# Splitting mixer outputs beside the retention's matmuls instead of in a stage of their own

## The chip, the cores and the metric

The kernel runs on one core of a Trainium2 chip, as one launch. The metric is the device time of that launch in microseconds (us). A core has TensorE (matmuls), VectorE, ScalarE, GpSimd (POOL in the profile) and SyncE (SP, which here only starts transfers). They run side by side and meet only through semaphores.

## The reference, cut to what matters

Two model blocks run one after the other on x of 256 positions by 2048 channels. The first has two layers, and the change lies in these:

```python
for l in range(DEPTH):                       # DEPTH = 2
    u = rms_norm(h, norm_pre_mix[l])
    p = u @ w_in[l]
    p_ret, p_hgrn, p_ml, p_rw = split_cols(p, GROUP_COLS)
    o_ret = retention_group(p_ret)           # 512 channels each
    o_hgrn = hgrn2_group(p_hgrn, ...)
    o_ml = mlstm_group(p_ml, ...)
    o_rw, v_first = rwkv7_group(p_rw, ...)
    mixed = concatenate([o_ret, o_hgrn, o_ml, o_rw]) @ w_out[l]
    h = h + rms_norm(mixed, norm_post_mix[l])
    h = h + rms_norm(gated_ffn(h), norm_post_ffn[l])   # width 5632

def retention_group(p):
    q, k, v, g = split_cols(p, RET_SPLIT)
    o = chunked_retention(rotary(q), rotary(k) * HEAD_DIM ** -0.5, v)
    return head_rms(o) * silu(g)
```

All is float32. The second block (attention of two kinds, 2048 wide) is not touched.

## The kernel before

**Products in two parts.** Every large product is made from rounded numbers and their remainders. ScalarE copies a slab of weights to `w_hi` in a rounded format, then VectorE or GpSimd writes `w_lo`, the weights less `w_hi`. The activations are treated in the same way: `x_hi` (ScalarE) and `x_lo` (VectorE) are the two halves of `x_parts`, 16 tiles of 128 channels by 256 positions. TensorE adds hi times hi, hi times lo and lo times hi. "To split" below means this.

**Layout.** Channels lie on the 128 partitions, positions along the free dimension. Weight slabs come through a ring of four slots (`weight_ring`), filled by SyncE. `Linear` is a product with the machine to itself: chunks of four output tiles, its weight split one slab ahead, its epilogue on ScalarE and VectorE. `Woven` is a product cut into pieces of nine matmuls, each piece half of a slab for one output tile. The stages of the four mixers place these pieces by hand between their own small matmuls. A list of shares says how many pieces go into each place: `plan` takes it, and `weave.pe`, `weave.act`, `weave.pool` and `weave.sp` issue what each engine has to do for the pieces up to a step. ScalarE's part is to round the weights (L552 and L564 for the halves of a slab, L185 for a whole one) and to read out finished output tiles (L622). GpSimd's part is the remainders (L555, L567, L193). A finished slab frees its slot of `w_hi` and `w_lo`, so each piece depends on what ScalarE and GpSimd did a few pieces before.

**Order around the change, in each layer.** rwkv, hgrn, mlstm and retention run in this order, each with its head norm at its end. During one mixer the input projection of the next is woven in. During retention it is the first part of the output product instead: `out_rest`, the rows of `w_out` that belong to hgrn, mlstm and rwkv (tiles 4 to 15 of `x_parts`), 16 slabs, 64 pieces. Its result is written to the arena. After retention's head norm `out_ret`, a `Linear` of one slab a chunk and four chunks, adds the product with retention's own 512 channels (tiles 0 to 3).

Each stage is a block. A block ends when all engines have drained; the last to be done holds the next. Before the change the sequence is:

1. mlstm's head norm, with the last pieces of retention's projection.
2. `split_stage`, a block of its own: three ScalarE copies and three VectorE subtractions of 128 by 1024 split the outputs of the three mixers.
3. `retention_stage`. SyncE loads the cosine and sine table (256 KB) and the decay table (1536 KB), then weights. TensorE rotates q and k (L1475), transposes v (L1447), does 8 woven pieces, and waits for `qk_ready` and `v_ready`. Then come the scores (L1428, L1430) and the weighted values, with 8 pieces after each of the four head pairs and 3 at the end. ScalarE begins with the second slab of `out_rest` (`weave.open`), then evacuates v. VectorE waits for the tables and makes q and k in three operations (L1515, L1517, L1518).
4. `head_norm_stage` of the retention: ScalarE squares, TensorE sums, ScalarE takes the root, VectorE inverts it and multiplies (L1411, L1413). Shares `[3, 64]`: 3 pieces before the sums, the rest (18) behind them. During the last of them ScalarE and GpSimd already split the first slab of `out_ret` (L185, L193).
5. `out_ret.run` with `lead=Split(...)`. ScalarE copies tiles 0 to 3 to `x_hi` (L898) and then splits the second slab. VectorE subtracts (L917). TensorE waits for that before its first matmul (L214).

Of the kernel before, what the change touches and what calls it, by code (L numbers as in the profile page):

```python
# [6 lines left out]
F32 = mybir.dt.float32  # L7
F32R = mybir.dt.float32r
I32 = mybir.dt.int32
ALU = mybir.AluOpType  # L10
ACT = mybir.ActivationFunctionType
# [7 lines left out]
GT = GW // P  # L19
# [10 lines left out]
EPS = 1e-6  # L30
# [3 lines left out]
class Signal:  # L34


    def __init__(self, ctx, nc, name):
        self.sem = ctx.enter_context(nc.semaphore(name))
        self.base = 0
        self.seen = 0  # L40
# [817 lines left out]
        core.end()  # L858


def split_stage(core, src, x0):

    nc = core.nc
    high = core.sig("x_high")
    quarters = range(0, src.shape[1], 4)
    with nc.Block() as block:
        @block.scalar
        def _(act):
            for n in quarters:
                nc.scalar.activation(core.x_hi[:, x0 + n:x0 + n + 4, :], src[:, n:n + 4, :], ACT.Copy).then_inc(*high.up())  # L870

        @block.vector
        def _(dve):
            for q, n in enumerate(quarters):
                dve.wait_ge(*high.at(q + 1))
                nc.vector.tensor_tensor(core.x_lo[:, x0 + n:x0 + n + 4, :], src[:, n:n + 4, :],
                                        core.x_hi[:, x0 + n:x0 + n + 4, :].bitcast(F32), ALU.subtract)
    core.end()


class Split:


    def __init__(self, m, sources, add=None):
        self.m, self.add = m, add
        self.src = [x[:, n:n + 4, :] for x in sources for n in range(0, x.shape[1], 4)]
        self.high, self.normed, self.ready = m.sig("x_high"), m.sig("normed"), m.sig("x_ready")
# [4 lines left out]
    def act(self, act, stream, first_split):  # L892

        m = self.m
        for q, x in enumerate(self.src):
            if self.add is not None:
                act.wait_ge(*self.normed.at(q + 1))
            m.nc.scalar.activation(m.x_hi[:, 4 * q:4 * q + 4, :], x, ACT.Copy).then_inc(*self.high.up())  # L898
            if q == 0:
                for g in range(first_split, 2):  # L900
                    stream.high(act, g)

    def dve(self, dve, stream, first_split):

        m, tt, n = self.m, self.m.nc.vector.tensor_tensor, len(self.src)

        def add(q):

            if self.add is not None and q < n:
                tt(self.src[q], self.src[q], self.add[:, 4 * q:4 * q + 4, :], ALU.add).then_inc(*self.normed.up())  # L910

        add(0)
        for q, x in enumerate(self.src):
            add(q + 1)
            at = slice(4 * q, 4 * q + 4)
            dve.wait_ge(*self.high.at(q + 1))
            tt(m.x_lo[:, at, :], x, m.x_hi[:, at, :].bitcast(F32), ALU.subtract).then_inc(*self.ready.up())  # L917
            if q == 0:
                for g in range(first_split, 2):
                    stream.low(dve, g)  # L920

# [426 lines left out]
        low(3)  # L1348


def head_norm_stage(m, o, dst, gate, weight=None, bias=None, bonus=None, eps=EPS, center=False, weave=Idle()):

    nc = m.nc
    sq = m.flat(S_AT, GT * T)
    inv = m.banks(0, 2)
    of = o.rearrange("p a b -> p (a b)")
    squares, sums, root = m.sig("squares"), m.sig("mean_sums"), m.sig("root")
    centred, mean = m.sig("centred"), m.sig("head_mean")
    flat = dst.rearrange("p a b -> p (a b)")
    with nc.Block() as block:  # L1360
        @block.tensor
        def _(pe):
            if center:
                for b in range(2):
                    mm = nc.tensor.matmul(m.ps[:, 2 + b, :], m.const("head_ones"), of[:, b * 512:(b + 1) * 512], start=True, stop=True)
                mm.then_inc(*mean.up())
            weave.pe(pe, 0)
            pe.wait_ge(*squares.at(1))
            for b in range(2):
                mm = nc.tensor.matmul(m.ps[:, b, :], m.const("head_ones"), sq[:, b * 512:(b + 1) * 512], start=True, stop=True)  # L1370
            mm.then_inc(*sums.up())
            weave.pe(pe, 1)

        @block.sync
        def _(sp):
            weave.sp(sp, 1)

        @block.gpsimd
        def _(pool):
            weave.pool(pool, 1)  # L1380

        @block.scalar
        def _(act):
            if center:
                act.wait_ge(*centred.at(1))
            nc.scalar.activation(sq, of, ACT.Square).then_inc(*squares.up())
            weave.act(act, 0)
            act.wait_ge(*sums.at(1))
            root_mean(m, m.banks(0, 2), inv, HD, eps).then_inc(*root.up())
            weave.act(act, 1)  # L1390

        @block.vector
        def _(dve):
            if center:

                dve.wait_ge(*mean.at(1))
                nc.vector.scalar_tensor_tensor(of, m.banks(2, 2), -1.0 / HD, of, ALU.mult, ALU.add).then_inc(*centred.up())
            if bonus is not None:
                for j in range(GT):
                    last = nc.vector.tensor_scalar(bonus[:, j, :], bonus[:, j, :], bias[:, j:j + 1], None, ALU.add)  # L1400
                done(dve, last, m.dve_step)
                done(dve, nc.vector.tensor_tensor(bonus, bonus, gate, ALU.mult), m.dve_step)
            dve.wait_ge(*squares.at(1))
            if weight is None:
                last = nc.vector.tensor_tensor(o, o, gate, ALU.mult)
            else:
                for j in range(GT):
                    last = nc.vector.scalar_tensor_tensor(o[:, j, :], o[:, j, :], weight[:, j:j + 1], gate[:, j, :], ALU.mult, ALU.mult)
            done(dve, last, m.dve_step)
            dve.wait_ge(*root.at(1))  # L1410
            done(dve, nc.vector.reciprocal(inv, inv), m.dve_step)  # L1411
            if bonus is None:
                nc.vector.tensor_tensor(flat, inv, of, ALU.mult)  # L1413
            else:
                done(dve, nc.vector.tensor_tensor(inv, inv, of, ALU.mult), m.dve_step)
                nc.vector.tensor_tensor(flat, inv, bonus.rearrange("p a b -> p (a b)"), ALU.add)
    m.end()
# [25 lines left out]
def transpose_values(pe, m, v, bank):  # L1443

    for tt in range(2):
        for j in range(GT):
            mm = m.nc.tensor.transpose(m.ps[:, bank + tt, j * P:(j + 1) * P], v[:, j, tt * P:(tt + 1) * P], m.const("ident"))  # L1447
    return mm


def retention_stage(m, p, weave):

    nc = m.nc
    q, k, v, g = (p.a(4 * n, GT) for n in range(4))
# [10 lines left out]
    with nc.Block() as block:  # L1465
# [7 lines left out]
        def _(pe):  # L1473
            for b in range(4):
                mm = nc.tensor.matmul(m.ps[:, b, :], m.const("rot_ret"), qk[:, b * 512:(b + 1) * 512], start=True, stop=True)  # L1475
            mm.then_inc(*rotated.up())
            transpose_values(pe, m, v, 4).then_inc(*v_turned.up())
            weave.pe(pe, 0)
            pe.wait_ge(*qk_ready.at(1))
            pe.wait_ge(*v_ready.at(1))  # L1480
# [18 lines left out]

        @block.scalar  # L1500
        def _(act):
            weave.open(act)
            act.wait_ge(*v_turned.at(1))
            nc.scalar.activation(vt, m.ps[:, 4:6, :], ACT.Copy).then_inc(*v_ready.up())
            nc.scalar.activation(g, g, ACT.Silu)
            weave.act(act, GT)
            act.wait_ge(*o_done.at(GT))
            nc.scalar.activation(q, m.banks(0, 2).rearrange("p (a b) -> p a b", b=T), ACT.Copy)
            weave.act(act, GT + 1)

        @block.vector
        def _(dve):
            turned = m.banks(0, 4).rearrange("p (a b) -> p a b", b=T)
            dve.wait_ge(*tables.all())
            done(dve, nc.vector.tensor_tensor(rot.rearrange("p (a b) -> p a b", b=T), p.a(0, 8), bcast(cs[:, 0:T], 8), ALU.mult), scaled)  # L1515
            dve.wait_ge(*rotated.at(1))
# [997 lines left out]
               [2, 1, 1, 1, 1, 1, 1, 1, 1], [2, 64])  # L2514
HGRN_SHARES = ([4] * 5 + [2, 1, 1, 1, 3] * GT + [0], [3, 68])
MLSTM_SHARES = ([6, 2, 7] + [6] * GT + [2], [2, 64])
RETENTION_SHARES = ([8] + [8] * GT + [3], [3, 64])


def first_block(m, a, after, landed, following, inputs):  # L2520
# [12 lines left out]
    for l in range(2):  # L2533
# [54 lines left out]
        ret.plan(MLSTM_SHARES[1])  # L2588
        head_norm_stage(m, m.a(P_AT, 4), m.a(MIX_AT + 8, 4), m.a(P_AT + 12, 4), vec(l, "mlstm_norm_w"), weave=ret)
        ret.end_weave()  # L2590
        split_stage(m, m.a(MIX_AT + 4, 12), 4)
        out_rest.begin_weave(out_ret)
        out_rest.plan(RETENTION_SHARES[0])
        retention_stage(m, there, out_rest)
        out_rest.plan(RETENTION_SHARES[1])
        head_norm_stage(m, there.a(0, 4), m.a(MIX_AT, 4), there.a(12, 4), weave=out_rest)
        out_rest.end_weave()
        post = Post(m, m.a(P_AT, 16), vec(l, "norm_post_mix"), m.a(MIX_AT, KT), m.a(60, 4), m.a(64, 4), reloaded)
        out_ret.run(gate_up, moves=reload, post=post, lead=Split(m, [m.a(MIX_AT, 4)]))

        lead = Lead(m, post, vec(l, "norm_pre_ffn"), m.a(MIX_AT, KT))
        ada_program, ada_move = ada_products(m, a["w_ada_2"][0], l, lead.ready.at(4))
# [744 lines left out]
```

## Time and profile before

| what | us |
|---|---|
| median of three runs | 3991.57 |
| the three runs | 3980.96, 3991.57, 3991.96 |
| the profiled execution | 3982.06 |
| its span | 3980.2 |
| TensorE busy in the span | 3676.9 (92%) |
| VectorE, ScalarE, GpSimd busy | 2032.0, 1772.9, 1734.3 |

The span reaches from the first to the last instruction of the profile; the device time has 1.9 us around it. Busy time of TensorE is modelled from pipelined matmuls, so two instructions in a row overlap: a woven matmul is listed with some 0.28 us and follows its forerunner by 0.12 us. L numbers are lines of the kernel. "PEclk" is the granted clock of TensorE as a share of full speed: 1.00 is 2.4 GHz and 0.50 is 1.2 GHz.

### The profile page before, as it was taken

The page shows a single profiled execution, that of the slowest core. Times are in us where ns is not written, and L with a number is a line of the kernel's source. Part 1 is how long each engine was busy: PE and PEld are TensorE (multiplying, and loading weights), DVE is VectorE, ACT ScalarE, POOL GpSimd, SP SyncE. Part 2 cuts the span into 40 slices and gives each one's busy share as a digit, 9 for nine tenths or more (in the row PEclk, how much of TensorE's full clock was granted, in tenths as well). Part 3 has the DMA queues.
Part 4 walks back from the last instruction along what each step waited for, and adds up shares of the span by engine and source line. Part 5 has one row for each costly group of instructions (what it writes and reads, how often), then busy time and mean ns, then how long its engine had stood idle before and what let it go on. Part 6 is the DMA issues. An engine that isn't in the chain of part 4 may idle for free. (4 is left out here: it accounts for less than half of the span.)

```text
span 3980.2 us, 60907 instructions
## 1 busy us (share of the span) xinstructions
PE 3676.9 (92%) x25724; PEld 3264.4 (82%) x25724; DVE 2032.0 (51%) x2013; ACT 1772.9 (45%) x1860; POOL 1734.3 (44%) x824
## 2 busy tenths in 40 slices
PE   8898899899999998898999799999998989889988
PEld 7788888688888887787888688888887788878877
DVE  5647522655555555646542555555555442344464
ACT  4416434544444444415444544443445345444433
POOL 0426565499992000325656399995000055440000
PEclk9899899999999999998999899999998999999999
DMA  5423335477775554423435477775554634335543
GB/s 189 139 63 123 119 123 193 142 243 243 236 240 180 185 188 132 143 66 112 130 120 164 148 239 242 246 235 188 190 183 156 192 109 122 112 124 186 167 157 120
DMA packets 378828, 655.47 MB, mean 165 GB/s; under 512 B 13713, under 2 KB 189921, under 8 KB 377745
## 3 DMA queue, kind: packets, MB, share of 16 engines
q1 hardware_dynamic: 363248, 596.98, 46.3%
q0 software_dynamic: 15392, 55.79, 4.1%
q8 instruction: 142, 2.33, 0.3%
q14 instruction: 46, 0.37, 0.0%
HBM read 645.37 MB, written 6.29 MB: 164 GB/s over the span
## 5 line engine op out<-in xcount | busy, mean ns | idle before, releaser
L214 PE MATMUL ps<-x_parts,w_hi 128*128 128x512 f32 x6160 | 2189.7, 400 | 95.1 <-DVE x_parts L1313 25.1
L215 PE MATMUL ps<-x_parts,w_lo 128*128 128x256 f32 x6160 | 1737.5, 282 | 0.0
L214 PEld LDWEIGHTS ps<-x_parts,w_hi 128*128 128x128 f32 x6160 | 1169.3, 190 | 383.0 <-issue 71.4
L193 DVE TENSOR_TENSOR w_lo<-weight_ring,w_hi 128x2048 fp32r<-128x2048 f32 x392 | 951.1, 2427 | 1039.1 <-ACT w_hi L185 1039.1
L185 ACT ACTIVATE w_hi<-weight_ring 128x2048 fp32r<-128x2048 f32 (+1 forms) x412 | 787.7, 1912 | 1169.6 <-PE ps L215 1110.3
L215 PEld LDWEIGHTS ps<-x_parts,w_lo 128*128 128x128 f32 x6160 | 1177.5, 191 | 0.0
L604 PE MATMUL ps<-x_parts,w_hi 128*128 128x256 f32 x2592 | 783.6, 302 | 67.4 <-ACT arena L622 33.5
L605 PE MATMUL ps<-x_parts,w_hi 128*128 128x256 f32 x2592 | 749.0, 289 | 0.0
L606 PE MATMUL ps<-x_parts,w_lo 128*128 128x256 f32 x2592 | 747.5, 288 | 0.0
L604 PEld LDWEIGHTS ps<-x_parts,w_hi 128*128 128x128 f32 x2592 | 513.0, 198 | 99.1 <-issue 58.9
L555 POOL TENSOR_TENSOR w_lo<-weight_ring,w_hi 128x1024 fp32r<-128x1024 f32 (+1 forms) x152 | 373.9, 2460 | 354.8 <-ACT w_hi L552 347.5
L605 PEld LDWEIGHTS ps<-x_parts,w_hi 128*128 128x128 f32 x2592 | 513.9, 198 | 4.6 <-issue 3.6
L606 PEld LDWEIGHTS ps<-x_parts,w_lo 128*128 128x128 f32 x2592 | 513.0, 198 | 0.0
L567 POOL TENSOR_TENSOR w_lo<-weight_ring,w_hi 128x1024 fp32r<-128x1024 f32 (+1 forms) x152 | 353.4, 2325 | 276.8 <-ACT w_hi L564 261.8
L2710 POOL TENSOR_SCALAR spare<-spare,second_vectors 128x512 f32<-128x512 f32 x180 | 418.9, 2334 | 3.9
L2714 POOL TENSOR_TENSOR arena<-arena,spare 128x512 f32<-128x512 f32 x180 | 365.3, 2030 | 14.6
L193 POOL TENSOR_TENSOR w_lo<-weight_ring,w_hi 128x2048 fp32r<-128x2048 f32 (+1 forms) x20 | 91.3, 4565 | 608.2 <-ACT w_hi L185 608.2
L552 ACT ACTIVATE w_hi<-weight_ring 128x1024 fp32r<-128x1024 f32 (+1 forms) x152 | 154.2, 1015 | 274.0 <-PE ps L606 274.0
L564 ACT ACTIVATE w_hi<-weight_ring 128x1024 fp32r<-128x1024 f32 (+1 forms) x152 | 154.3, 1015 | 210.4 <-PE ps L606 197.9
L115 POOL DMA_DIRECT2D spare<-in_w_ada x96 | 73.5, 765 | 160.7 <-POOLq L375 75.3
L115 POOL DMA_DIRECT2D arena<-in_w_ck x4 | 3.3, 826 | 302.7 <-DVE w_lo L193 302.7
L3085 DVE SCALAR_TENSOR_TENSOR arena<-ps,arena 128x256 f32<-128x256 f32 (+1 forms) x40 | 20.4, 553 | 163.6 <-PE ps L2991 130.2
(405 smaller groups left out, 2847.5 us busy)
## 6 DMA issues: line engine op xcount, KB each, us to landing
weight_ring<-in_w_in SPq DMA_DIRECT2D x212, 1024.0 KB, 5.2
weight_ring<-in_w_ffn_gate SPq DMA_DIRECT2D x88, 1024.0 KB, 5.3
weight_ring<-in_w_ffn_up SPq DMA_DIRECT2D x88, 1024.0 KB, 5.3
weight_ring<-in_w_ffn_down SPq DMA_DIRECT2D x88, 1024.0 KB, 5.2
spare<-in_w_ada POOLq DMA_DIRECT2D x96, 512.0 KB, 4.5
weight_ring<-in_w_out SPq DMA_DIRECT2D x32, 768.0 KB, 4.6
weight_ring<-in_w_out SPq DMA_DIRECT2D x24, 1024.0 KB, 5.1
weight_ring<-in_w_br_a SPq DMA_DIRECT2D x8, 1024.0 KB, 5.1
```

Source lines behind the costliest of these rows:

```text
L185: core.nc.scalar.activation(core.w_hi[:, g % 2, at], core.ring[:, (self.start + g) % RING, at], ACT.Copy)\
L193: (ops or core.nc.vector).tensor_tensor(core.w_lo[:, g % 2, at], core.ring[:, (self.start + g) % RING, at], core.w_hi[:, g % 2, at].bitcas ...
L214: mm(out, hi, core.x_parts[:, x, :, :].rearrange("p a t -> p (a t)"), start=first, stop=False)
L215: return mm(out[:, 0:T], lo, core.x_hi[:, x, :], start=False, stop=last)
L555: core.nc.gpsimd.tensor_tensor(lo, src, hi.bitcast(F32), ALU.subtract).then_inc(core.upper_low.sem, 1)
L564: core.nc.scalar.activation(hi, src, ACT.Copy).then_inc(core.hi_ready, 1)
L567: core.nc.gpsimd.tensor_tensor(lo, src, hi.bitcast(F32), ALU.subtract).then_inc(core.lo_ready, 1)
L604: mm(out, hi, x_hi, start=(kk == 0), stop=False)
L605: mm(out, hi, x_lo, start=False, stop=False)
L606: last = mm(out, lo, x_hi, start=False, stop=(kk == 2 * self.ks - 1))
L2710: ins = nc.gpsimd.tensor_scalar(to, buf[:, n % 2, k, :], c[:, 2 * s + k:2 * s + k + 1], None, ALU.mult)
L2714: done(pool, nc.gpsimd.tensor_tensor(out, out, buf[:, n % 2, k, :], ALU.add), step)
```

## The change

`split_stage` goes away. `Split`, which until now only led a `Linear`, gets a first tile `x0` and may be used without a weight stream. Retention's block calls it first on ScalarE and VectorE, and TensorE waits for all three parts ahead of its first woven piece. The head norm of the retention gets a `Split` as well: ScalarE does it between two portions of woven pieces, behind `normed`, and VectorE behind its last product. The shares `[3, 64]` become `[3, 9, 64]`. `out_ret.run` has no lead any more.

```diff
-def split_stage(core, src, x0):
...
 class Split:
-    def __init__(self, m, sources, add=None):
+    def __init__(self, m, sources, add=None, x0=0):
+        self.at = [slice(x0 + 4 * q, x0 + 4 * q + 4) for q in range(sum(x.shape[1] for x in sources) // 4)]
...
-            m.nc.scalar.activation(m.x_hi[:, 4 * q:4 * q + 4, :], x, ACT.Copy).then_inc(*self.high.up())
-            if q == 0:
+            m.nc.scalar.activation(m.x_hi[:, self.at[q], :], x, ACT.Copy).then_inc(*self.high.up())
+            if q == 0 and stream is not None:
                 for g in range(first_split, 2):
                     stream.high(act, g)
...
 def head_norm_stage(..., weave=Idle(), split=None):
+    last_step = 1 if split is None else 2
...
-            weave.pe(pe, 1)
+            for n in range(1, last_step + 1):
+                weave.pe(pe, n)
...
-            weave.sp(sp, 1)
+            weave.sp(sp, last_step)
...
-            weave.pool(pool, 1)
+            weave.pool(pool, last_step)
...
             root_mean(m, m.banks(0, 2), inv, HD, eps).then_inc(*root.up())
             weave.act(act, 1)
+            if split is not None:
+                act.wait_ge(*normed.at(1))
+                split.act(act, None, 2)
+                weave.act(act, last_step)
...
-                nc.vector.tensor_tensor(flat, inv, of, ALU.mult)
+                nc.vector.tensor_tensor(flat, inv, of, ALU.mult).then_inc(*normed.up())
+                if split is not None:
+                    split.dve(dve, None, 2)
...
 def retention_stage(m, p, weave, split):
             transpose_values(pe, m, v, 4).then_inc(*v_turned.up())
+            pe.wait_ge(*split.ready.at(len(split.src)))
             weave.pe(pe, 0)
...
+            split.act(act, None, 2)
             weave.open(act)
...
+            split.dve(dve, None, 2)
             dve.wait_ge(*tables.all())
...
-RETENTION_SHARES = ([8] + [8] * GT + [3], [3, 64])
+RETENTION_SHARES = ([8] + [8] * GT + [3], [3, 9, 64])
...
-        split_stage(m, m.a(MIX_AT + 4, 12), 4)
-        retention_stage(m, there, out_rest)
+        retention_stage(m, there, out_rest, Split(m, [m.a(MIX_AT + 4, 12)], x0=4))
-        head_norm_stage(m, there.a(0, 4), m.a(MIX_AT, 4), there.a(12, 4), weave=out_rest)
+        head_norm_stage(m, there.a(0, 4), m.a(MIX_AT, 4), there.a(12, 4), weave=out_rest, split=Split(m, [m.a(MIX_AT, 4)]))
-        out_ret.run(gate_up, moves=reload, post=post, lead=Split(m, [m.a(MIX_AT, 4)]))
+        out_ret.run(gate_up, moves=reload, post=post)
```

## Rows read from the trace of the kernel before

**Rows 1.** The page, busy time of each engine (share of the span, instructions).
```profile
PE 3676.9 (92%) x25724; PEld 3264.4 (82%) x25724; DVE 2032.0 (51%) x2013; ACT 1772.9 (45%) x1860; POOL 1734.3 (44%) x824
```

**Rows 2.** Waits of TensorE, whole span: total us, times, longest.
```profile
PE ps L214 <- DVE x_parts L917: 24.3, 4, 7.6
...
PE ps L1475 <- PEq L866: 11.2, 2, 5.6
```

**Rows 3.** Timeline, layer 0, retention's start: start us, us, engine, line, operation, [idle before].
```profile
589.30 2.95 ACT L870 ACTIVATE x_parts<-arena 128x1024 fp32r<-128x1024 f32 x3 [0.28 <-PEq L1360]
590.39 3.50 DVE L876 TENSOR_TENSOR x_parts<-arena,x_parts 128x1024 fp32r<-128x1024 f32 x3 [23.43 <-ACT x_parts L870]
...
594.19 6.43 PE L1475 MATMUL ps<-h,small_consts 128*128 128x512 f32 x8 [5.59 <-PEq L866]
...
595.73 3.42 POOL L193 TENSOR_TENSOR w_lo<-weight_ring,w_hi 128x1536 fp32r<-128x1536 f32 x1 [7.78 <-ACT w_hi L185]
...
600.46 1.04 PE L1447 MATMUL ps<-small_consts,h 128*128 128x128 f32 x8
...
600.95 2.29 DVE L1515 TENSOR_TENSOR arena<-h,arena 128x2048 f32<-128x2048 f32 x1 [7.07 <-DMA arena<-in_consts]
...
601.25 0.36 PE L604 MATMUL ps<-x_parts,w_hi 128*128 128x256 f32 x1
...
605.61 2.29 DVE L1518 TENSOR_TENSOR h<-ps,arena 128x2048 f32<-128x2048 f32 x1
...
610.04 0.70 PE L1428 MATMUL ps<-h 64*128 64x256 f32 x4
```

**Rows 4.** Stretches of that timeline: busy us (count) by engine, PEclk, DMA share, GB/s.
```profile
594.17:596.00 1.83, 1.81 (x2) 0.82 (x3) 0.00 (x0) 1.48 (x1) 0.27 (x1) 0.50 0.41 78
...
600.00:601.50 1.50, 1.50 (x12) 1.18 (x11) 0.55 (x1) 0.00 (x0) 0.00 (x0) 1.00 0.94 333
```

**Rows 5.** Timeline, layer 1, the same place.
```profile
2102.65 3.75 PE L1475 MATMUL ps<-h,small_consts 128*128 128x512 f32 x4 [5.59 <-PEq L866]
...
2109.88 2.29 DVE L1515 TENSOR_TENSOR arena<-h,arena 128x2048 f32<-128x2048 f32 x1 [7.53 <-DMA arena<-in_consts]
...
2118.62 0.70 PE L1428 MATMUL ps<-h 64*128 64x256 f32 x4
```

**Rows 6.** Timeline, layer 0, end of the head norm and start of `out_ret`.
```profile
669.18 1.23 DVE L1413 TENSOR_TENSOR arena<-ps,h 128x1024 f32<-128x1024 f32 x1
...
671.04 0.38 ACT L622 ACTIVATE arena<-ps 128x256 f32<-128x256 f32 x1 [0.23 <-PE ps L606]
...
672.87 0.37 ACT L622 ACTIVATE arena<-ps 128x256 f32<-128x256 f32 x1
...
678.81 4.56 POOL L193 TENSOR_TENSOR w_lo<-weight_ring,w_hi 128x2048 fp32r<-128x2048 f32 x1 [3.93 <-ACT w_hi L185]
...
683.83 1.06 ACT L898 ACTIVATE x_parts<-arena 128x1024 fp32r<-128x1024 f32 x1 [2.31 <-PEq L1360]
...
686.29 0.76 PE L214 MATMUL ps<-x_parts,w_hi 128*128 128x512 f32 x1 [5.19 <-DVE x_parts L917]
```

**Rows 7.** The last stretch behind that start in which PEclk is below 1.00.
```profile
690.00:692.00 2.00, 2.00 (x8) 1.68 (x7) 0.00 (x0) 0.00 (x0) 0.00 (x0) 0.52 0.90 355
```

**Rows 8.** Timeline, layer 0, head norm's start: VectorE and GpSimd at once.
```profile
655.71 1.85 POOL L555 TENSOR_TENSOR w_lo<-weight_ring,w_hi 128x768 fp32r<-128x768 f32 x1 [1.70 <-POOLq L1465]
...
656.80 1.84 DVE L1405 TENSOR_TENSOR h<-h 128x1024 f32<-128x1024 f32 x1 [13.27 <-ACT arena L1386]
...
658.00 2.32 POOL L567 TENSOR_TENSOR w_lo<-weight_ring,w_hi 128x768 fp32r<-128x768 f32 x1 [0.45 <-ACT w_hi L564]
```

**Rows 9.** Stretches around two other gaps of TensorE of 2.7 to 2.8 us.
```profile
310.50:313.30 2.80, 0.07 (x1) 0.10 (x2) 2.39 (x2) 0.47 (x2) 0.82 (x1) 0.95 0.00 0
313.30:316.50 3.20, 3.20 (x16) 3.20 (x17) 0.70 (x1) 3.17 (x3) 1.30 (x1) 0.51 0.68 199
...
2058.00:2066.00 8.00, 5.28 (x37) 4.36 (x35) 6.59 (x5) 4.17 (x5) 4.01 (x2) 1.00 0.11 24
```

More of the change, by code:

```diff
@@ L858, in run @@
         core.end()
-def split_stage(core, src, x0):
[L863 to L878, printed above, removed]
 class Split:
-    def __init__(self, m, sources, add=None):
+    def __init__(self, m, sources, add=None, x0=0):
+        self.at = [slice(x0 + 4 * q, x0 + 4 * q + 4) for q in range(sum(x.shape[1] for x in sources) // 4)]
         self.m, self.add = m, add
@@ L914, in dve @@
             add(q + 1)
-            at = slice(4 * q, 4 * q + 4)
+            at = self.at[q]
             dve.wait_ge(*self.high.at(q + 1))
             tt(m.x_lo[:, at, :], x, m.x_hi[:, at, :].bitcast(F32), ALU.subtract).then_inc(*self.ready.up())
-            if q == 0:
+            if q == 0 and stream is not None:
                 for g in range(first_split, 2):
@@ L1348, in dve, with head_norm_stage @@
         low(3)
-def head_norm_stage(m, o, dst, gate, weight=None, bias=None, bonus=None, eps=EPS, center=False, weave=Idle()):
+def head_norm_stage(m, o, dst, gate, weight=None, bias=None, bonus=None, eps=EPS, center=False, weave=Idle(), split=None):
     nc = m.nc
@@ L1357, in head_norm_stage @@
     squares, sums, root = m.sig("squares"), m.sig("mean_sums"), m.sig("root")
-    centred, mean = m.sig("centred"), m.sig("head_mean")
+    centred, mean, normed = m.sig("centred"), m.sig("head_mean"), m.sig("normed")
     flat = dst.rearrange("p a b -> p (a b)")
+    last_step = 1 if split is None else 2
     with nc.Block() as block:
@@ L1448, in transpose_values, with retention_stage @@
     return mm
-def retention_stage(m, p, weave):
+def retention_stage(m, p, weave, split):
     nc = m.nc
```

## The prediction

> **What bounds the kernel now.** I read the page first, to see which engine fills the span. TensorE is busy for 92% of it [rows 1], so a change pays by what it takes out of TensorE's gaps. Then I took the list of waits, restricted to TensorE, to see which gap belongs to the edited lines. Two do: TensorE stands still 5.6 us at L1475, held by the block of the split (L866), and the products of L214 wait for the halves of L917, 24.3 us in four places [rows 2], two of which are this change's. Last came the timelines of both places and the granted clock in them. Each place occurs once in each of the first part's two layers.
>
> At the retention's start the reader is to see this [rows 3]. The block of the split begins at 589.30: three ScalarE copies end at 592.25, three VectorE subtractions end at 593.89, and TensorE has nothing. The retention's block starts at 594.19. TensorE then needs 6.27 us for the rotation (L1475), 0.79 us for the transposes (L1447), and 8.79 us for eight woven pieces, up to L1428 at 610.04. VectorE meanwhile waits for the tables until 600.95 and does three operations until 607.90. TensorE comes 2.14 us after that, so it is TensorE that sets the pace here, and not VectorE. The clock stands at 0.50 in that rotation, after a gap of 5.59 us, and is back at 1.00 from 600.00 [rows 4].
>
> At the head norm's end [rows 6] GpSimd finishes the first slab of the next product (L193) at 683.37, ScalarE begins the new block at 683.83, and it and VectorE split the retention's output. TensorE starts at 686.29. Here too the clock is at half afterwards, up to the end of the stretch 690 to 692 [rows 7].
>
> **The change, part one: the split moves into the retention's block.** Call that block's start s. It moves from 594.19 to where the split block began: 589.32, so by 4.87 us. In layer 1 the gap in front of L1475 is the same 5.59 us, so the shift is too [rows 3, 5]. From s on:
>
> ScalarE does its three copies first, to s+2.95. The high half of the second slab, which took 1.5 us before GpSimd could start (595.73 against 594.19), comes behind them. GpSimd's L193 so runs from s+4.5 to s+7.9 (3.42 us). VectorE's three subtractions end at s+4.6 (1.09 until the first starts, 3.50 for all).
>
> TensorE needs none of this for rotation and transposes. Its gap shrinks from 5.6 us to about 0.7, so I take the clock to stay at 1.00: about 5.6 us of the rotation ran at half, which gives 2.8 us back. The rotation becomes 3.45 us, with the transposes 4.25. It then waits 0.35 us for the split (new wait, at s+4.6), and the eight pieces end at s+13.4. Behind that wait in its queue stand only the pieces; nobody waits for them at once. Without the clock's return it would be s+15.85, as now.
>
> VectorE waits for the tables as before, since both table transfers are SyncE's first in the block and move with s. They land at s+6.76 in layer 0 and s+7.23 in layer 1 (594.19 to 600.95, 2102.65 to 2109.88). So the three subtractions cost nothing: the wait for the tables hides them, with 2.2 us to spare. Without that cover they would cost up to 3.5 us. What is late next is L1515. It reads two tensors of SBUF while GpSimd's L193 now still runs; before, GpSimd had ended by 599.15. The nearest rows are VectorE's L1405, two such inputs, 1.84 us while GpSimd's L555 still had 0.76 us to run, against 1.23 us for L1413 of the same size with one input in PSUM. The delay is 0.6 us, most of the 0.76, and the next GpSimd operation, L567, is longer in its turn, 2.32 us [rows 6, 8]. L1515 asks at s+6.76 with 1.2 us of L193 left: delay 1.1 us (layer 1: 0.6). The bounds are nothing and the whole rest, 1.2. I take 1.1 because the row shows nearly the whole rest. The chain of three takes 6.95 us (600.95 to 607.90), so qk is ready at s+14.8 in both layers, which is now later than the pieces (s+13.4). TensorE goes on at s+14.85, against 15.85 before (15.97 in layer 1, 2118.62 less 2102.65). Gain: 4.87 + 1.0 = 5.9 us, and 4.87 + 1.1 = 6.0 us. Sum of part one: 11.9 us.
>
> The Trainium skill (SBUF — State Buffer, section Who interferes with whom) speaks against the change here: a VectorE operation with two SBUF inputs and a GpSimd operation reading SBUF exclude each other for the whole instruction, whoever starts first. By that rule the delay is 1.2 and 0.7 us, the sum 0.2 us smaller; with no such conflict it would be 1.7 us larger. The trace's L1405 agrees with the rule roughly (0.6 of 0.76).
>
> Bounds of part one: without the delay of L1515 13.6 us. At the low end the tables land 2 us later: nothing in the rows says so, but the landing is now on the path and the loads of w_out share the queue; with the block's shift alone and that, (4.87 + 1.0 - 2) x 2 = 7.7 us.
>
> **Part two: the split of the retention's own output moves into the head norm.** `normed` is raised by L1413, which ends at 670.41. ScalarE has done its work of the first nine pieces at 671.42 (L622). So it does not wait, by 1.0 us. Its copy of 1.06 us (L898) [rows 6] pushes the next half slab and the next L622 back: that one ends at 673.7 and not at 673.24, and TensorE's next pieces, which write the bank that it reads, start 0.45 us later. Everything behind it follows, GpSimd's L193 too: the new block begins with ScalarE at 684.28. VectorE's subtraction lies in idle time. The program of SyncE is the same, in two portions.
>
> In the new block TensorE waits for nobody and starts at 684.28, not 686.29: 2.0 us. ScalarE and VectorE split the second slab 1.3 us sooner after the block's start than before. Then the clock. The gap before was 5.2 us and the clock was at half for 5.7 us afterwards, 2.8 us lost. Now it is 2.7 us (TensorE ended at 681.1, now 681.55). The nearest rows disagree: after 2.8 us at 310.5 the clock stood at 0.51 for 3.2 us, a loss of 1.6; between 2058 and 2066 TensorE was idle 2.7 of 8 us and the clock stayed at 1.00 [rows 9]. Of five gaps of 2.5 to 2.8 us that I looked at, four were followed by a fall, so I take the fall: 1.2 us gained. Bounds: no gain in clock, and all 2.8. Part two is 3.2 us a layer, 6.4 in all, between 4.0 and 9.6. Nothing behind it eats this up: chunk two of that product waits for the epilogue of the first, which moves with it.
>
> **Sum.** 11.9 + 6.4 = 18.3 us. The profiled execution took 3982.06 us (span 3980.2), so 3963.8 by its own time. It was near the fastest of the three runs; the median, 3991.57, is 9.5 us above it. I let the gain off the median: 3973.3 us, 0.46% less; I write 3973.
>
> **Rivals.**
> (1) The strong form: L1515 isn't delayed and the clock stays up in both places. 13.6 + 9.6 = 23.2 us, 3968 us. For it: the gap without a fall [rows 9]. Against it: L1405 [rows 8]. Chance 0.12.
> (2) The weak form: the tables land later now that they are on the path, and the second gap still costs the full stretch of half clock. 7.7 + 4.0 = 11.7 us, 3980 us, at the edge of 0.3%, which is 12 us and about what a measurement of this kernel can tell from no change. For it: SyncE's queue fills with w_out right behind the tables, and the three runs already differ by 11 us. Against: the old landing was measured under the same load. Chance 0.25.
> (3) Slower: ScalarE's new wait for `normed`. It stands ahead of the half slab and the reads of nine woven pieces. If VectorE's reciprocal and product came later than 671.42, TensorE would stall as long behind L622. The margin is 1.0 us. The gain is used up at (18.3 / 2) + 1.0 = 10.2 us of lateness per layer, and at 16.2 us of it, 6 more per layer, the kernel takes 3991.57 + 12 = 4004 us, slower by 0.3%. For it: that this is the only new wait with no cover of its own. Against: the chain that leads to it begins with the same root and is not touched. Chance 0.04.
> (4) The change doesn't act as described (another block edge holds the retention back by as much): no change, 3992. Chance 0.03.
> The forecast itself, 15 to 21 us: 0.56; its own range is 3970 to 3977.
>
> **Range and chances.** The terms' bounds give 11.7 to 23.2 us. The median may also sit at the other end of the 11 us in which the runs lie, so I add 5 us above and 11 below: 3957 to 3985. Faster by over 0.3%: the forecast, the strong form and a third of the weak, 0.76. Slower: 0.04. The rest, 0.20, is the same.
>
> **What would show it.** No block between the last woven L606 and L1475, with a gap under 1 us and the clock at 1.00 behind it; L1447 ending 4.3 us after the block's start; VectorE's chain ending last before L1428, and L1515 longer than 2.29 us or not; in the head norm L898's copy at about the time that the ninth piece is read, with no idle time charged to `normed`; the first L214 of w_out within 0.3 us of its block's start, and a shorter stretch of half clock. The prediction is wrong if L1428 comes later than s+15.5, if the clock falls in the rotation all the same, or if the gap before L214 stays over 3.5 us.

## The result, and the profile after

The changed kernel takes 3967.89 us (median of five runs, 3960.19 to 3973.74) against 3990.92 us before (five runs, 3980.96 to 3991.96). The ratio is 0.995 with a 95% interval of 0.9936 to 0.9964: faster by 0.5%, between 14 and 26 us. Put on a chip once more, beside two experiments, it gave 0.9949 (0.9935 to 0.9963). Its profiled execution has a span of 3958.4 us, 21.8 us less than before.

The list of TensorE's waits, whole span (total us, times, longest), answers to [rows 2]:

```profile
PE ps L214 <- DVE x_parts L898: 13.9, 2, 7.6
...
PE ps L214 <- ACTq L428: 10.9, 4, 4.1
...
PE ps L1417 <- DVE h L1510: 2.6, 2, 1.3
...
PE ps L1464 <- PEq L1342: 1.5, 2, 0.7
```

The wait of 11.2 us for the split's block is now 1.5 us at L1464, the rotation. The waits for the split's halves are two instead of four. Two entries are new: 1.3 us a layer for L1510, the last of VectorE's three operations in front of the scores, and two more gaps charged to ScalarE's queue at a block's start (L428: four gaps and 10.9 us, before two and 5.4 us). These two are the gaps in front of the next product. Line numbers are those of the changed kernel: L879 and L898 are the split's copy and subtraction, L1507 to L1510 VectorE's chain, L1417 the first scores.

The retention's start in layer 0, the changed kernel's timeline (start, duration, engine, line, operation, idle before), against [rows 3]:

```profile
586.39 2.95 ACT L879 ACTIVATE x_parts<-arena 128x1024 fp32r<-128x1024 f32 x3 [0.28 <-PEq L1342]
586.41 1.95 PE L1464 MATMUL ps<-h,small_consts 128*128 128x512 f32 x4 [0.73 <-PEq L1342]
...
587.48 3.50 DVE L898 TENSOR_TENSOR x_parts<-arena,x_parts 128x1024 fp32r<-128x1024 f32 x3 [23.43 <-ACT x_parts L879]
...
589.92 1.04 PE L1436 MATMUL ps<-small_consts,h 128*128 128x128 f32 x8
...
590.79 3.56 POOL L193 TENSOR_TENSOR w_lo<-weight_ring,w_hi 128x1536 fp32r<-128x1536 f32 x1 [5.76 <-ACT w_hi L185]
...
591.03 0.19 PEld L604 LDWEIGHTS ps<-x_parts,w_hi 128*128 128x128 f32 x1 [0.31 <-DVE x_parts L898]
...
593.82 2.69 DVE L1507 TENSOR_TENSOR arena<-h,arena 128x2048 f32<-128x2048 f32 x1 [2.84 <-DMA arena<-in_consts]
...
598.87 2.29 DVE L1510 TENSOR_TENSOR h<-ps,arena 128x2048 f32<-128x2048 f32 x1
...
601.22 0.70 PE L1417 MATMUL ps<-h 64*128 64x256 f32 x4 [1.31 <-DVE h L1510]
```

ScalarE, VectorE and TensorE now work in the same block, which begins at 586.4. The rotation takes 3.5 us (586.41 to 589.92) and not 6.3: it runs at full clock, as the stretch from 586.4 to 591 shows (columns as in [rows 4]):

```profile
586.40:591.00 4.60, 4.54 (x16) 2.36 (x16) 3.50 (x3) 4.32 (x5) 0.20 (x1) 1.00 0.80 283
```

TensorE starts its woven pieces at 591.03, after 0.31 us of waiting for the split. L1507 starts while GpSimd's L193 runs (to 594.35) and takes 2.69 us, 0.40 longer than before. GpSimd pays too: its next operation, L555, begins at 595.21 and takes 3.02 us, 1.85 before. VectorE's chain ends at 601.16, and TensorE waits for it. In layer 1 the tables land sooner behind the block's start, L1507 meets more of L193 and is longer, and the scores still come at the same distance (2095.86 less the block's first matmul at 2081.06 is 14.80 us):

```profile
2087.80 3.35 DVE L1507 TENSOR_TENSOR arena<-h,arena 128x2048 f32<-128x2048 f32 x1 [2.17 <-DMA arena<-in_consts]
...
2095.86 0.70 PE L1417 MATMUL ps<-h 64*128 64x256 f32 x4 [1.30 <-DVE h L1510]
```

The head norm's end in layer 0, the changed kernel's timeline, against [rows 6]:

```profile
660.36 1.22 DVE L1400 TENSOR_TENSOR arena<-ps,h 128x1024 f32<-128x1024 f32 x1
...
662.21 0.38 ACT L622 ACTIVATE arena<-ps 128x256 f32<-128x256 f32 x1 [0.23 <-PE ps L606]
662.50 1.05 ACT L879 ACTIVATE x_parts<-arena 128x1024 fp32r<-128x1024 f32 x1
663.44 0.83 ACT L564 ACTIVATE w_hi<-weight_ring 128x768 fp32r<-128x768 f32 x1
663.58 1.41 DVE L898 TENSOR_TENSOR x_parts<-arena,x_parts 128x1024 fp32r<-128x1024 f32 x1 [2.00 <-ACT x_parts L879]
664.18 0.38 ACT L622 ACTIVATE arena<-ps 128x256 f32<-128x256 f32 x1
664.36 2.34 POOL L567 TENSOR_TENSOR w_lo<-weight_ring,w_hi 128x768 fp32r<-128x768 f32 x1 [0.45 <-ACT w_hi L564]
...
670.12 4.56 POOL L193 TENSOR_TENSOR w_lo<-weight_ring,w_hi 128x2048 fp32r<-128x2048 f32 x1 [3.43 <-ACT w_hi L185]
...
675.18 0.77 PE L214 MATMUL ps<-x_parts,w_hi 128*128 128x512 f32 x1 [2.77 <-ACTq L428]
```

ScalarE's copy (662.50) follows the read of the ninth piece without a wait. The product's first matmul comes with its block. The gap in front of it is 2.77 us, from 672.41 on: for 2.27 us of it GpSimd's L193 still runs, to 674.68, and 0.50 us pass from there to the first matmul of the new block. Behind the gap the clock is at half for some 3.3 us:

```profile
675.10:677.00 1.90, 1.82 (x5) 1.59 (x6) 0.00 (x0) 1.86 (x1) 0.00 (x0) 0.50 0.80 147
677.00:679.00 2.00, 2.00 (x9) 1.73 (x8) 1.91 (x1) 0.06 (x1) 0.00 (x0) 0.62 0.84 336
679.00:681.00 2.00, 2.00 (x14) 1.74 (x13) 0.38 (x1) 0.00 (x0) 0.00 (x0) 1.00 1.03 434
```

The time of a whole run moves by more than some of these effects, so all kernels are compared below by distances within the profile, in layer 0 / layer 1:

- A: from the last read of retention's projection (L622, at 588.63 and 585.72 here) to the first scores
- B: from there to the head norm's product of the gate (VectorE, 128x1024 in 1.84 us; L1405 before)
- C: from there to the next product's first matmul (L214)
- D: from there to ScalarE's third slab of that product, which waits for its first chunk of outputs and so shows how long the chunk took

| kernel | A | B | C | D |
|---|---|---|---|---|
| before | 21.41 / 21.52 | 46.76 / 46.75 | 29.49 / 29.49 | 8.45 / 8.47 |
| after | 15.50 / 15.48 | 46.75 / 46.74 | 27.21 / 27.21 | 7.36 / 7.39 |
| after, again | 15.49 / 15.49 | 46.75 / 46.75 | 27.21 / 27.21 | 7.31 / 7.15 |

A gives 5.9 and 6.0 us, C 2.3 and 2.3, D 1.1 and 1.1: 18.7 us. Of the 21.8 us by which the two spans differ, 2.9 lay ahead of the first edited place (588.63 against 585.72), where nothing was changed. That is the spread between runs: in the other profiles the same read lies anywhere from 583.87 to 590.86.

D is the least steady of the four. Behind the gap of 5.19 us it was 8.45, 8.47, 7.86, 8.54, 7.70 and 8.32 us in the three profiles that have that gap. Behind the gap of 2.77 us it was between 7.15 and 7.45 us in eight of twelve cases, 5.83 in three and 8.66 in one, as the profiles below show. The means are 8.22 and 6.92 us.

### The profile page after: what moved, and what is told of

It is laid out like the page before. It is cut to its first block and busy times, and to the rows that moved or that the text cites. A ratio compares the mean times of both kernels' runs of the same rounds, so it can differ in the third digit from the quotient of the medians.

```text
span 3958.4 us, 60887 instructions
## 1 busy us (share of the span) xinstructions
PE 3662.7 (93%) x25724; PEld 3249.1 (82%) x25724; DVE 2039.9 (52%) x2013; ACT 1771.8 (45%) x1860; POOL 1729.3 (44%) x824
## 5 line engine op out<-in xcount | busy, mean ns | idle before, releaser
L214 PE MATMUL ps<-x_parts,w_hi 128*128 128x512 f32 x6160 | 2191.0, 400 | 89.8 <-DVE x_parts L1294 25.4
L193 DVE TENSOR_TENSOR w_lo<-weight_ring,w_hi 128x2048 fp32r<-128x2048 f32 x392 | 950.1, 2424 | 1057.0 <-ACT w_hi L185 1056.8
L214 PEld LDWEIGHTS ps<-x_parts,w_hi 128*128 128x128 f32 x6160 | 1169.3, 190 | 382.3 <-issue 60.9
L555 POOL TENSOR_TENSOR w_lo<-weight_ring,w_hi 128x1024 fp32r<-128x1024 f32 (+1 forms) x152 | 377.8, 2485 | 340.7 <-ACT w_hi L552 333.5
L193 POOL TENSOR_TENSOR w_lo<-weight_ring,w_hi 128x2048 fp32r<-128x2048 f32 (+1 forms) x20 | 91.5, 4576 | 602.2 <-ACT w_hi L185 602.2
```

The lines of the kernel that those rows point to most:

```text
L193: (ops or core.nc.vector).tensor_tensor(core.w_lo[:, g % 2, at], core.ring[:, (self.start + g) % RING, at], core.w_hi[:, g % 2, at].bitcas ...
L214: mm(out, hi, core.x_parts[:, x, :, :].rearrange("p a t -> p (a t)"), start=first, stop=False)
L555: core.nc.gpsimd.tensor_tensor(lo, src, hi.bitcast(F32), ALU.subtract).then_inc(core.upper_low.sem, 1)
```

## Experiments

The theory is that of the prediction: two places, each a removed stretch of idle TensorE plus the clock behind it, the first capped by VectorE's chain and GpSimd's operation in it, the second by GpSimd's first slab. The rivals were that the gain is chance, that the clock has no part in it, and that the tables' landing and not GpSimd's operation is what caps the first place.

### Each part alone

The first run leaves out the head norm's `split`, with `[3, 64]` and the `lead` as before. The second keeps `split_stage` and the retention's block as they were.

```diff
-        head_norm_stage(m, ..., weave=out_rest, split=Split(m, [m.a(MIX_AT, 4)]))
+        head_norm_stage(m, ..., weave=out_rest)
-        out_ret.run(gate_up, moves=reload, post=post)
+        out_ret.run(gate_up, moves=reload, post=post, lead=Split(m, [m.a(MIX_AT, 4)]))
```

> Only part one is done: the three mixers' split lies in the retention's block, the retention's own output is split by the lead of the next product as before. Theory: part one is worth 5.9 and 6.0 us in the two layers, 11.9 us in all, so about 3979 us against 3991 (ratio 0.997). L1428's counterpart stands 14.85 us behind the block's start, as in the changed kernel, and the first matmul of the next product is still preceded by a gap of 5.2 us with half clock for 5.7 us behind it. Rival (the gain is mostly the clock falling elsewhere by chance): under 5 us.

> Only part two is done: the split block stays, the retention's own output is split inside its head norm with shares 3, 9, 64. Theory: 3.2 us a layer, 6.4 us in all, about 3984.5 us (ratio 0.998); gap in front of the first matmul 2.8 us instead of 5.2, half clock behind it for 3.3 us instead of 5.7 or not at all. Rival (ScalarE's copy in the middle of the weave eats the gain): no change in the distance from the head norm's start to the end of the product's first chunk.

| kernel | ratio to before (95%) | A | C | D |
|---|---|---|---|---|
| part one alone | 0.9976 (0.9965 to 0.9987) | 15.50 / 15.49 | 29.48 / 29.47 | 7.86 / 8.54 |
| part two alone | 0.9982 (0.9969 to 0.9996) | 21.32 / 20.24 | 27.20 / 27.19 | 7.43 / 7.41 |

The two ratios give 9.6 and 7.2 us of 3987. A and C belong to one part each: C is as before with part one alone, A is the whole change's, and the other way round with part two alone. So both parts are real, and neither needs the other. One number stands out: with part two alone A is 20.24 us in layer 1, where the kernel before has 21.52. The gap is the same 5.59 us, but the granted clock was at 0.50 for 3.2 us behind it (2104.8 to 2108.0), in the kernel before for 5.8 us (2102.65 to some 2108.5). That layer's clock differed, not the work.

### The clock in the rotation

```diff
 def split_stage(core, src, x0):
...
     with nc.Block() as block:
+        @block.tensor
+        def _(pe):
+            for n in range(5):
+                nc.tensor.matmul(core.ps[:, 5, :], core.const("head_ones"), src[:, 2 * n:2 * n + 2, :].rearrange("p a b -> p (a b)"), start=True, stop=True)
...
```

> The kernel before, with five float32 matmuls of 512 columns added to the split block, whose result nobody reads (extra work, output unchanged). Only the clock should differ. Theory (half of part one's reserve is the clock): the rotation runs at 1.00, TensorE reaches its woven pieces 4.3 us after the block's start, VectorE's chain ends at 13.7 us and L1428 comes there instead of at 15.85: 2.1 us a layer, 4.2 us in all (ratio 0.999). Rival (the clock is no part of the gain, only the removed block is): L1428 stays at 15.85 and nothing is gained.

The run's timeline, layer 0 (L1481 is the rotation there, L1434 the first scores):

```profile
589.42 3.67 PE L1481 MATMUL ps<-h,small_consts 128*128 128x512 f32 x8 [0.34 <-PEq L866]
...
603.28 0.70 PE L1434 MATMUL ps<-h 64*128 64x256 f32 x4 [0.69 <-DVE h L1524]
```

The scores stand 13.86 us (13.80 in layer 1) behind the block's start and not 15.85: 2.0 and 2.2 us (layer 1: 15.97) from useless matmuls alone. The rotation takes 3.67 us with them, 6.43 without. The ratio was 0.9988 (0.9976 to 1.0), which by itself hardly tells 4 us from nothing; the distances do. So here the idle stretch costs its length and the slow rotation behind it, and TensorE's wait of 0.69 us for VectorE's chain takes back part of what the clock gives.

### GpSimd's operation against VectorE's

Two runs attack the cap from both sides. The first swaps ScalarE's order in the retention's block:

```diff
-            split.act(act, None, 2)
             weave.open(act)
+            split.act(act, None, 2)
```

> The changed kernel with ScalarE's order in the retention's block swapped: the second slab's high half first, the three copies of the split behind it. Theory (VectorE's operations with two SBUF inputs and GpSimd's exclude each other): GpSimd's L193 now runs from 1.6 to 5.1 us behind the block's start and VectorE's first subtraction, due at 2.6, is stretched until 5.1, so the split is ready only at about 7.5 to 8.5 us instead of 4.6; TensorE starts its pieces there and L1428's counterpart comes at 16.5 to 17 us instead of 14.8; L1515's counterpart is no longer stretched (2.29 us). Rival (no exclusion): subtractions of 1.2 us each ready at 6.1 us, L1428 at 14.9, no change.

```profile
591.41 3.46 POOL L193 TENSOR_TENSOR w_lo<-weight_ring,w_hi 128x1536 fp32r<-128x1536 f32 x1 [2.92 <-ACT w_hi L185]
...
592.31 3.64 DVE L898 TENSOR_TENSOR x_parts<-arena,x_parts 128x1024 fp32r<-128x1024 f32 x1 [24.82 <-ACT x_parts L879]
...
598.14 2.28 DVE L1507 TENSOR_TENSOR arena<-h,arena 128x2048 f32<-128x2048 f32 x1
598.27 0.29 PEld L604 LDWEIGHTS ps<-x_parts,w_hi 128*128 128x128 f32 x1 [4.10 <-DVE x_parts L898]
```

The first subtraction starts under L193 and takes 3.64 us where it takes 1.17 alone; L193 ends at 594.87 and the subtraction 1.08 us later. TensorE gets its pieces 8.4 us behind the block's start (its matmuls after 3.85 us idle, its weight loads after the 4.10 us of the row), and the scores come at 19.5 us (18.7 in layer 1). That is worse than the 17 us expected, and half clock follows this gap too: PEclk is 0.50 from 598.25 to 602. L1507, which GpSimd no longer meets, takes 2.28 us, with the DMA engines busy all the while (share 1.10 from 598.25 to 600), so it is not the transfers that lengthen it. This kernel was run once, and only its distances are used.

The second run lets VectorE start L1507 as soon as it can:

```diff
-            tables.start(sp, decay, m.const_dram("ret_decay")...)
+            decays.start(sp, decay, m.const_dram("ret_decay")...)
...
             nc.vector.tensor_tensor(qk, m.banks(0, 4), rot, ALU.add).then_inc(*qk_ready.up())
+            dve.wait_ge(*decays.all())
```

> The changed kernel, but VectorE's rotation waits only for the cosine and sine table (256 KB); the decay table (1536 KB) is waited for ahead of the first scores. Theory (GpSimd's operation sets L1507's end, and the landing only hides in front of it): L1507 now starts at 4.6 us behind the block's start, is stretched until GpSimd's L193 is done at 8.0 us and ends at 10.2; the chain ends at 14.8 and TensorE's first scores stay at 14.85 us. Rival (the landing alone is what is late): the chain ends at 11.6 us, TensorE does not wait any more and the scores start at 13.45, 1.4 us earlier in each layer.

```profile
590.33 3.55 POOL L193 TENSOR_TENSOR w_lo<-weight_ring,w_hi 128x1536 fp32r<-128x1536 f32 x1 [5.76 <-ACT w_hi L185]
590.43 5.60 DVE L1507 TENSOR_TENSOR arena<-h,arena 128x2048 f32<-128x2048 f32 x1
...
600.74 0.70 PE L1417 MATMUL ps<-h 64*128 64x256 f32 x4 [1.30 <-DVE h L1510]
```

L1507 starts 2.9 us earlier, takes 5.60 us instead of 2.69, and the scores are where they were (14.79 us). It is the same in layer 1. The rival is out: not the landing sets the time, but GpSimd's operation. (This kernel, too, was run once.) The rule of the Trainium skill (SBUF — State Buffer, section Who interferes with whom), that the two block each other for a whole instruction, fits this row: 590.33 + 3.55 + 2.29 is 596.17, and L1507 ends at 596.03.

### The gap in front of the next product

Three runs on the 2.77 us. One fills them with three useless matmuls behind the last woven piece. One gives the next product's first slab to VectorE (the flag that keeps GpSimd from doing it is left out here):

```diff
+    def first_low(self, dve):
+        self.reached(dve, self.core.lo_ready, self.n_slabs - 1)
+        self.after.low(dve, 0)
...
                     split.dve(dve, None, 2)
+                    weave.first_low(dve)
```

> The changed kernel with three float32 matmuls of 512 columns (2.6 us, result read by nobody) behind TensorE's last woven piece of the retention's head norm, where it stands idle for 2.8 us. Only the clock should differ. Theory: no half clock behind the gap, the first chunk of the next product takes 5.8 us instead of 7.4 in layer 0; about 1.6 us a layer. Rival (the clock behind that gap is not tied to the gap): the first chunk still takes 7.4 us.

> The changed kernel, but the remainder of the next product's first slab is made by VectorE (2.3 us) and not by GpSimd (4.56 us) at the end of the head norm. Theory (the gap of 2.8 us in front of the next product is GpSimd's operation, after TensorE has ended): the gap shrinks to about 0.7 us, no half clock behind it: 2.1 + 1.6 = 3.7 us a layer, 7.5 us in all (ratio to the kernel before 0.993). Rival (another engine holds the block's end, or the clock falls all the same): under 3 us.

With the filler D is 5.82 / 5.92 us instead of 7.36 / 7.39, and C 27.46, 0.25 us later: the clock alone is worth 1.5 us a layer there. With the slab on VectorE the gap is 0.88 us and the clock stays up. C is 25.31 / 25.32, D 5.93 / 5.93, so 3.3 us a layer less, against 3.7 expected. The ratios to the kernel before are 0.9927 (0.9913 to 0.9940) with the filler and 0.9928 (0.9915 to 0.9942) with the slab on VectorE. They don't tell the two apart, though by the distances the filler gives 1.3 us a layer and the slab on VectorE 3.3; the changed kernel itself did not run beside them. The timeline of the run with the slab on VectorE, that slab and TensorE's first matmul:

```profile
674.42 2.29 DVE L193 TENSOR_TENSOR w_lo<-weight_ring,w_hi 128x2048 fp32r<-128x2048 f32 x1 [5.16 <-ACT w_hi L185]
...
677.56 0.47 PE L214 MATMUL ps<-x_parts,w_hi 128*128 128x512 f32 x1 [0.88 <-ACTq L428]
```

The third makes the prediction's slower rival real: `[3, 4, 64]`.

> The changed kernel with shares 3, 4, 64 instead of 3, 9, 64: ScalarE reaches its wait for the normed output after four pieces, before VectorE has it. Theory: ScalarE stands at the wait for about 4 us (the prediction's slower rival made real), its half slabs and reads come up to 3.7 us late, and TensorE's pieces behind it lose 1 to 2 us a layer against 3, 9, 64 (0.45 us late there). Rival (the wait is covered wherever it is put): no loss.

```profile
660.07 1.06 ACT L879 ACTIVATE x_parts<-arena 128x1024 fp32r<-128x1024 f32 x1 [3.96 <-DVE arena L1400]
...
674.63 0.47 PE L214 MATMUL ps<-x_parts,w_hi 128*128 128x512 f32 x1 [2.77 <-ACTq L428]
...
680.46 1.92 ACT L185 ACTIVATE w_hi<-weight_ring 128x2048 fp32r<-128x2048 f32 x1 [3.95 <-PE ps L215]
```

ScalarE stands 3.96 us at the wait, and C is 28.20 / 28.21: 1.0 us a layer lost. So the place of the second portion matters, but three quarters of ScalarE's wait does not reach the next product. That weights already split absorb it is likely and was not tested. The rows show something else as well. The gap is the same 2.77 us, yet the first chunk takes 5.83 us here: the clock did not fall (PEclk 1.00 from 674.60 to 681). In layer 1 it fell for long (8.66 us). With ScalarE's order swapped, above, the gap was again 2.77 us and D 5.83 us in both layers. Whether the clock falls behind such a gap is open from one run to the next. So the filler's 5.82 / 5.92 us in one profile could be chance too; together with the slab on VectorE and the two kernels below there are eight cases without the long gap, and the clock fell in none, against nine of twelve with it.

### Both caps at once

Both kernels here start from the run with the next product's first slab on VectorE. The first adds a woven piece ahead of the scores, as in the diff. The second has eight pieces there as before; in it VectorE also makes the second slab's remainder in the retention's block, the tables are waited for apart, and the head norm's shares are `[3, 10, 64]`.

```diff
-RETENTION_SHARES = ([8] + [8] * GT + [3], [3, 9, 64])
+RETENTION_SHARES = ([9] + [8] * GT + [3], [3, 9, 64])
```

> The run with the next product's first slab on VectorE, and besides one woven piece more ahead of the scores (shares 9, 8, 8, 8, 8, 3 and 3, 9, 64), to fill TensorE's wait of 1.3 us for VectorE's chain. Theory: the scores stay at 14.8 us behind the block's start, so the piece costs nothing there and is missing (1.08 us) behind the sums; ScalarE's copy of the split also comes one piece later and no longer delays a read (0.45 us). 3.3 + 1.1 + 0.45 = 4.8 us a layer against the changed kernel, 9.7 in all, ratio to the kernel before 0.992. Rival (the ninth piece waits for its half slab or its bank and pushes the scores back): 3.3 us a layer or less.

> The other way round TensorE's wait: the next product's first slab on VectorE as before, and in the retention's block VectorE also makes the second slab's remainder, ahead of its chain, and waits only for the cosine and sine table there, so that it never meets GpSimd; shares 3, 10, 64. Theory: subtractions end at 4.6, the slab at 6.4, the chain at 13.3 us; L1507 takes 2.29 us; TensorE ends its eight pieces at 13.4 and the scores start at 13.45 instead of 14.8: 1.4 + 3.3 + 0.45 = 5.1 us a layer against the changed kernel, 10.3 in all, ratio to the kernel before 0.992. Rival (tables or something else than GpSimd's operation sets the chain): scores at 14 us or later.

> The changed kernel once more, on the same chip as the two before, to have them side by side: 0.5% under the kernel before, and the distances of both edited places as in its first profile (15.5 us from the last read to the scores, 27.2 us from the head norm's product to the next product's first matmul). The clock behind that gap of 2.8 us falls or doesn't, as chance has it.

| kernel | median us | ratio to before (95%) | A | B | C | D |
|---|---|---|---|---|---|---|
| first slab on VectorE, ninth piece | 3958.87 | 0.9919 (0.9906 to 0.9932) | 15.49 / 15.49 | 47.44 / 47.44 | 24.10 / 24.10 | 5.82 / 5.82 |
| both slabs on VectorE | 3961.25 | 0.9927 (0.9914 to 0.9939) | 14.14 / 14.12 | 46.75 / 46.75 | 25.17 / 25.16 | 5.93 / 5.92 |
| after, again | 3971.84 | 0.9949 (0.9935 to 0.9963) | see above | | | |

The ninth piece leaves the scores where they are and shortens C by 1.2 us against the slab on VectorE alone, but B grows by 0.7: over half of it is given back. The profile shows where. At the block's edge between retention and head norm TensorE stands 0.98 us, with the slab on VectorE alone 0.30. With one piece shifted, GpSimd has a half slab more to finish at that edge, and it ends last:

```profile
646.75 1.83 POOL L557 TENSOR_TENSOR w_lo<-weight_ring,w_hi 128x768 fp32r<-128x768 f32 x1 [1.32 <-ACT w_hi L554]
...
648.92 0.36 PE L606 MATMUL ps<-x_parts,w_hi 128*128 128x256 f32 x1 [0.98 <-PEq L1462]
```

This is read from the rows; no run moves that half slab. The second variant does in the retention's block what was expected of it: scores at 13.45 and 13.44 us behind the block's start, L1507's counterpart (L1518 here) 2.28 us long behind a slab of 1.75 us.

```profile
590.11 1.75 DVE L193 TENSOR_TENSOR w_lo<-weight_ring,w_hi 128x1536 fp32r<-128x1536 f32 x1
...
591.78 2.28 DVE L1518 TENSOR_TENSOR arena<-h,arena 128x2048 f32<-128x2048 f32 x1
```

By A to D it is 4.8 and 4.9 us a layer under the changed kernel, where 5.1 were expected, the other 4.0 where 4.8 were; the share of one piece more (`[3, 10, 64]`) brought only 0.15 of the 0.45 us. The two medians don't order them, their intervals overlap. Both beat the kernel before. The changed kernel on the same chip, 3971.84 us, is beaten by the first clear of both intervals; the second's interval touches it, and there the distances decide.

## Why the prediction was right

The predicted 3973 us lies 5 us above the measured median, which is inside the range, and the direction and the size (18.3 us forecast, 23.0 by the medians, 14 to 26 by the interval) hold. Step by step:

- **The block's shift, 4.87 us.** TensorE's gap fell from 5.59 to 0.73 us, 4.86 us.
- **The clock in the rotation.** Kept at 1.00, rotation and transposes in 4.3 us where 4.25 stood. The prediction took it that a gap of 0.7 us is not followed by a fall, without a row for it; none followed here. The filler run shows the clock as a cause, 2.0 and 2.2 us.
- **The split hidden by the tables' wait.** TensorE reached its pieces 4.6 us behind the start, after 0.31 us at the new wait (0.35 forecast).
- **L1515's delay.** Right as a mechanism, off in the layers: 0.40 and 1.06 us against 1.1 and 0.6. The tables landed at 7.41 and 6.74 us this time, not 6.76 and 7.23. It made no difference, since GpSimd's end sets the chain's: L1507 ends 2.16 us behind GpSimd's L193 in layer 0 and 2.15 in layer 1 (596.51 against 594.35, 2091.15 against 2089.00). The scores came at 14.81 and 14.80 us; 14.85 stood in the prediction.
- **Part two.** 2.3 us for the start (2.0 forecast) and 1.1 for the clock (1.2). That the clock's term came so close is in part luck: in three of twelve cases with that gap the clock did not fall, and in one it fell for much longer. The term that was too large is ScalarE's copy: it made the following read 0.1 us late, not 0.45 (664.18 less 647.97 is 16.21 us behind the head norm's product of the gate, 672.87 less 656.80 was 16.07). The prediction set the operations end to end, but in the rows each of ScalarE's begins 0.1 us ahead of the end of the one in front: the copy (662.50 against 662.21 + 0.38), the half slab (663.44 against 662.50 + 1.05) and the next read (664.18 against 663.44 + 0.83). These three overlaps are 0.29 us, about the whole of what 0.45 was too much.
- **The rivals.** The strong form fell with L1507. The weak form's late tables came by 0.65 us in layer 0 and cost nothing. The slower one needs ScalarE at its wait before VectorE, which the share of nine avoids; when made real it costs 1.0 us a layer for a wait of 3.96 us, so the prediction's account of it, us for us, was too dear.
- **From the profile to the median.** The sum of the terms is 18.3, the two places gave 18.7, the medians 23. What is left lies outside the edited places and is within the spread below. No term of the forecast stood for it, so how close 3973 came to the median is in part luck.

## What to carry to other kernels

In this kernel a block of a few microseconds that left TensorE idle cost its length and a slow stretch behind it (4.9 and 2.0 us); look at the granted clock on both sides of a gap before pricing its removal, and then at which engine's chain becomes last. A transfer's wait is good cover for VectorE only as long as GpSimd doesn't read SBUF at the moment when it ends: a VectorE operation with two SBUF inputs that met one took 5.60 us instead of 2.29, and started 2.9 us later it ended no later. At a block's end ask which engine is last to finish; giving its last operation to an engine that was idle there gave 3.3 us a layer for a few lines, against 9.3 of the whole change.

## What the runs showed of the hardware that had not been expected

Two profiles of the same changed kernel differ by 12.4 us, and the distances A and C in them are equal to 0.01 us. TensorE is busy for 3662.7 us in the one and 3678.5 in the other with the same instructions, and the mean granted clock differs (each from the view of the cores: before, after, after again):

```profile
core 0: 3980.2 us, clock 0.960
```

```profile
core 0: 3958.4 us, clock 0.965
```

```profile
core 0: 3970.8 us, clock 0.962
```

The mean granted clock is lower by 0.003, which is 0.6% of the span more at half clock, some 24 us. If TensorE sets the pace there, half of it is lost: 12 us, and between 8 and 16 as the means are rounded. That is about the whole of the difference. Over the 49 executions of the kernel before that ran beside the experiments, from 3976.40 to 4002.94 us, the slower ones also have the lower clock (correlation -0.71). So the spread between runs of this kernel goes in good part with how often and how long the clock falls behind gaps that are the same in each run; that nothing else adds to it is not shown. A gap of 2.77 us was followed by a first chunk of 7.36 us in one run, of 5.83 in another and of 8.66 in a third case.
